# The last column block of a down projection in two passes by token tiles, on one core of a Trainium2 chip

## The reference, cut to what matters

```python
gate, up = jnp.split(h @ w_gu, 2, axis=-1)
f = (jax.nn.silu(gate) * up) @ w_down          # (640, 5632) @ (5632, 2048)
x = layer_norm(ALPHA * x + g2 * f, ln2_g, ln2_b)
# layer_norm: mean and variance over the 2048 columns of a token, then
# (x - mean) * rsqrt(var + eps) * g + b
```

## Time and profile before

| what | value |
|---|---|
| time, median of 3 runs | 2842.35 us (2841.35 to 2844.21) |
| profiled execution, its own time | 2838.47 us |
| its span, first to last instruction | 2836.7 us |
| busy: PE, DVE, ACT, POOL | 95%, 48%, 32%, 24% |
| a round of the down projection | 13.60 us, 44 of them |
| from the end of the last product to the end of the span | 31.2 us |

### The profile page before, as it was taken

How to read it: one execution, slowest core, us unless ns; L and a number is a source line. 1 busy time by engine, 2 the same in 40 slices (tenths; PEclk the granted TensorE clock), 3 DMA queues, 4 the chain that set the end, 5 groups by cost and what they waited for, 6 DMA issues and landing times.

```text
span 2836.7 us, 37630 instructions
## 1 busy us (share of the span) xinstructions
PE 2702.8 (95%) x16256; PEld 2412.5 (85%) x16256; DVE 1367.9 (48%) x1564; ACT 893.9 (32%) x933; POOL 680.5 (24%) x227
## 2 busy tenths in 40 slices
PE   5798999999998998999999999999999999999995
PEld 2577887879986885999999999999999888888884
DVE  5222232325566447555555555545555544445445
ACT  5222232323222116333333333333333322332231
POOL 0000000000000010444444444444433433333331
PEclk8999999999999997999999999999999999999998
DMA  8864545641346322223333332223333646454642
GB/s 328 316 238 176 184 170 198 212 150 58 106 150 238 101 74 103 86 94 98 103 104 104 104 103 88 94 95 104 104 104 122 245 180 220 171 204 168 217 167 104
DMA packets 164681, 424.50 MB, mean 150 GB/s; under 512 B 9484, under 2 KB 11924, under 8 KB 157476
## 3 DMA queue, kind: packets, MB, share of 16 engines
q1 hardware_dynamic: 162212, 416.84, 42.4%
q10 hardware_dynamic: 2304, 5.24, 0.5%
HBM read 388.20 MB, written 33.85 MB: 149 GB/s over the span
## 4 chain that ended last, share of the span: by engine, by line
PE 68%; DVE 9%; POOL 9%; DMA 8%; issue 3%; ACT 3%; SPq 0%; POOLq 0%; ACTq 0%; DVEq 0%
PE ps L1972 7%; PE ps L1974 7%; PE ps L1973 7%; PE ps L1947 6%; PE ps L1949 6%; PE ps L1948 6%; PE ps L1668 5%; PE ps L1670 5%; PE ps L1669 5%; DMA raw_w<-w_gu_b 4%; PE ps L1721 4%; POOL raw_w L785 3%; PE ps L1648 3%; DVE w_lo L1402 2%; POOL low L782 2%
## 5 line engine op out<-in xcount | busy, mean ns | idle before, releaser
L1402 DVE TENSOR_TENSOR w_lo<-raw_w,w_hi 128x1024 fp32r<-128x1024 f32 x264 | 332.7, 1260 | 295.6 <-ACT w_hi L1034 292.5
L1034 ACT ACTIVATE w_hi<-raw_w 128x1024 fp32r<-128x1024 f32 x264 | 269.5, 1054 | 604.9 <-POOL raw_w L791 367.8
L1947 PE MATMUL ps<-x_hi,w_hi 128*128 128x320 f32 x1408 | 437.2, 310 | 10.8 <-DVE w_lo L1402 8.9
L1948 PE MATMUL ps<-x_lo,w_hi 128*128 128x320 f32 x1408 | 436.7, 310 | 0.0
L1949 PE MATMUL ps<-x_hi,w_lo 128*128 128x320 f32 x1408 | 436.5, 310 | 0.0
L782 POOL TENSOR_TENSOR low<-raw_w 128x1024 f32<-128x1024 f32 x44 | 110.5, 2512 | 1052.4 <-DMA raw_w<-w_gu_b 926.1
L1512 DVE TENSOR_TENSOR x_lo<-low,x_hi 128x2560 fp32r<-128x2560 f32 x44 | 216.2, 4915 | 289.8 <-ACT x_hi L1100 289.8
L1668 PE MATMUL ps<-x_hi,w_hi 128*128 128x320 f32 x1056 | 341.7, 324 | 8.2 <-DVE x_lo L1206 6.2
L1972 PE MATMUL ps<-w_hi,x_hi 128*128 128x512 f32 x880 | 342.7, 389 | 2.4 <-POOL w_lo L796 2.4
L1974 PE MATMUL ps<-w_hi,x_lo 128*128 128x512 f32 x880 | 342.6, 389 | 0.0
L1973 PE MATMUL ps<-w_lo,x_hi 128*128 128x512 f32 x880 | 342.5, 389 | 0.0
(11 more groups left out here) (194 smaller groups left out, 4338.8 us busy)
## 6 DMA issues: line engine op xcount, KB each, us to landing
raw_w<-w_gu_b SPq DMA_DIRECT2D x176, 512.0 KB, 5.6
low<-w_ada SPq DMA_DIRECT2D x60, 1024.0 KB, 5.4
low<-hidden_scratch SPq DMA_DIRECT2D x44, 1280.0 KB, 6.0
raw_w<-w_down SPq DMA_DIRECT2D x44, 1024.0 KB, 5.1
raw_w<-w_in_b SPq DMA_DIRECT2D x33, 1024.0 KB, 7.4
high<-w_ada SPq DMA_DIRECT2D x22, 1024.0 KB, 5.3
raw_w<-w_out SPq DMA_DIRECT2D x16, 1024.0 KB, 5.1
x_raw<-w_ada SPq DMA_DIRECT2D x14, 1024.0 KB, 9.3
```

The source lines that it names most:

```text
L1034: nc.scalar.activation(weight(0, n), quad(W_OF[i]), ACT.Copy).then_inc(prod_hi, 1)
L1402: nc.vector.tensor_tensor(weight(1, n), quad(W_OF[n % 7]), weight(0, n).bitcast(F32), ALU.subtract).then_inc(prod_split, 1)
L1947: mm(prod_bank(n), wh, version(v, 0, k), start=k == 0, stop=False)
L1948: mm(prod_bank(n), wh, version(v, 1, k), start=False, stop=False)
```

## The change

The fourth column block is computed in two passes over the 11 groups. The first pass (rounds 33 to 43, LAST_A to LAST_B) takes token tiles 0 to 2, the second (rounds 44 to 54) tiles 3 and 4. There are 55 rounds in place of 44: the weight tiles of the block are loaded and split twice, the activation tiles in part each time (384 columns, then 256).

- In the second pass DVE makes `w_lo` (`late_rest`) in place of POOL, which splits up to round 44.
- While the second pass runs, the layer norm of tiles 0 to 2 is done: DVE evacuates tile 2 and makes the scale and the shift of the three (`scale_of`), ACT takes the roots and normalises the tiles (`tail_normalise`, one 128 x 2048 instruction each), and POOL multiplies by the gain and adds the bias (two 128 x 2048 instructions each, six in all). SP stores them after its last load.
- Tiles 3 and 4 are normalised on DVE after the last product, in halves of 1024 columns, and stored in halves.
- Gain and bias rows go into the free columns of the activation ring, loaded in round 37.

```diff
+N_DOWN = 5 * N_DG
+LAST_A, LAST_B = 3 * N_DG, 4 * N_DG
+TAIL = 3
+def down_unit(j):
+    b, g = divmod(j, N_DG)
+    return min(b, 3), g, ((0, TT), (0, TAIL), (TAIL, TT))[max(0, b - 2)]
...
+    x_rows = x_raw[:, 0:KT * T].rearrange("p (k c) -> p k c", c=T)
+    ln2_row = [x_rows[:, 8 * i:8 * i + 8, TAIL * P:T] for i in range(2)]
+    def folded_tile(t):
+        return u_acc[:, t, :].rearrange("p (k c) -> p k c", k=8)
...
         def load_down(j):
+            elif j - 2 <= LAST_B:
+                sp.wait_ge(split_done, FU + j - 1)
             else:
-                sp.wait_ge(split_done, FU + j - 1)
+                sp.wait_ge(late_split, j - 2 - LAST_B)
...
-        for t in range(TT):
-            sp.wait_ge(y_done, t + 1)
+        for t in range(TAIL):
+            sp.wait_ge(y_early, t + 1)
             sp.dma_start(y_t[t], u_acc[:, t, :]).then_inc(y_out, 16)
+        for t in range(TAIL, TT):
+            for i in range(2):
+                sp.wait_ge(y_done, 2 * (t - TAIL) + i + 1)
+                sp.dma_start(y_t[t][:, 1024 * i:1024 * i + 1024],
+                             u_acc[:, t, 1024 * i:1024 * i + 1024]).then_inc(y_out, 16)
...
     def _(pool):
-        for j in range(4 * N_DG):
+        for j in range(LAST_B + 1):
             s = (j + 1) % 2
             pool.wait_ge(down_hi, j + 1)
             nc.gpsimd.tensor_tensor(w_lo[:, s, :], raw_w[:, j % 2, :], w_hi[:, s, :].bitcast(F32),
                                     ALU.subtract).then_inc(split_done, 1)
+        pool.wait_ge(tail_rows_in, 32)
+        for t in range(TAIL):
+            tile = folded_tile(t)
+            pool.wait_ge(tail_normed, t + 1)
+            nc.gpsimd.tensor_tensor(tile, tile, ln2_row[0], ALU.mult).then_inc(y_gained, 1)
+            pool.wait_ge(y_gained, t + 1)
+            nc.gpsimd.tensor_tensor(tile, tile, ln2_row[1], ALU.add).then_inc(y_early, 1)
...
     def _(act):
+        for j in range(2, N_DOWN):
+            hid_round(j)
+            if j == LAST_B + 2:
+                tail_root(0)
+                tail_root(1)
+            if j > LAST_B + 2 and j - LAST_B - 3 < TAIL:
+                tail_normalise(j - LAST_B - 3)
+            down_round(j)
+            if j == LAST_B + 2:
+                tail_root(2)
...
     def _(dve):
+        def late_rest(j):
+            s = (j + 1) % 2
+            dve.wait_ge(down_hi, j + 1)
+            nc.vector.tensor_tensor(w_lo[:, s, :], raw_w[:, j % 2, :], w_hi[:, s, :].bitcast(F32),
+                                    ALU.subtract).then_inc(late_split, 1)
+        for nb in range(4):
+            for g in range(N_DG):
+                hid_rest(N_DG * nb + g + 2)
+                if g == 6:
+                    ready_rows(nb)
+            for t in range(TAIL - 1 if nb == 3 else TT):
+                evac_down(nb, t)
+        for j in range(LAST_B, N_DOWN):
+            if j + 1 < N_DOWN:
+                late_rest(j + 1)
+            if j == LAST_B:
+                evac_down(3, TAIL - 1)
+                scale_of(0)
+                scale_of(1)
+            if j == LAST_B + 1:
+                scale_of(2)
+            if j + 2 < N_DOWN:
+                hid_rest(j + 2)
+        for t in range(TAIL, TT):
+            evac_down(3, t)
...
+        for t in range(TAIL, TT):
+            tile = folded_tile(t)
...
+            for i in range(2):
+                part = slice(4 * i, 4 * i + 4)
+                link(nc.vector.scalar_tensor_tensor(tile[:, part], tile[:, part], mv(t, 0), ln2_row[0][:, part],
+                                                    ALU.subtract, ALU.mult))
+                nc.vector.scalar_tensor_tensor(tile[:, part], tile[:, part], mv(t, 2), ln2_row[1][:, part],
+                                               ALU.mult, ALU.add).then_inc(y_done, 1)
```

More of the change, by code:

```diff
@@ L748, in _ @@
         store_hid(FB - 2)
-        for j in range(4 * N_DG):
-            if j + 2 < 4 * N_DG:
+        for j in range(N_DOWN):
+            if j + 2 < N_DOWN:
                 load_hid(j + 2)
@@ L754, in _ @@
                 store_hid(FB - 1)
[L755 removed]
+            if j % N_DG == 2 and j < LAST_B:
                 load_down_rows(j // N_DG)
[L757 to L763 removed]
+            if j == LAST_A + 4:
+                sp.wait_ge(down_used, LAST_A)
+                for i in range(2):
+                    row = rows[4 + i:5 + i, :].rearrange("r (k c) -> r k c", k=8)
+                    sp.dma_start(ln2_row[i], row.to_broadcast([P, 8, 256])).then_inc(tail_rows_in, 16)
+        for t in range(TAIL):
+            sp.wait_ge(y_early, t + 1)
+            sp.dma_start(y_t[t], u_acc[:, t, :]).then_inc(y_out, 16)
+        for t in range(TAIL, TT):
[3 more added lines that the diff above has]
+                             u_acc[:, t, 1024 * i:1024 * i + 1024]).then_inc(y_out, 16)
+        sp.wait_ge(y_out, 16 * (2 * TT - TAIL))
     @block.gpsimd
@@ L1132, in _, with tail_root, tail_normalise @@
         down_round(1)
[L1133 to L1136, removed]
+        def tail_root(t):
             act.wait_ge(moments, TT + t + 1)
             nc.scalar.activation(mv(t, 2), mv(t, 1), ACT.Sqrt, bias=cols(C_EPS, 1)).then_inc(scaled, 1)
+        def tail_normalise(t):
+            act.wait_ge(tail_scale, t + 1)
+            nc.scalar.activation(u_acc[:, t, :], u_acc[:, t, :], ACT.Identity, bias=mv(t, 3),
+                                 scale=mv(t, 2)).then_inc(tail_normed, 1)
+        for j in range(2, N_DOWN):
[9 more added lines that the diff above has]
+        for t in range(TAIL, TT):
+            tail_root(t)
     @block.vector
@@ L1572, in stat2_of @@
             return stat2[:, t]
[L1574 to L1596, removed]
@@ L1597, in _, with ready_rows @@
+        def ready_rows(nb):
+            dve.wait_ge(down_gates_in, 80 * (nb + 1))
+            for i in range(2):
+                row = high[:, G_GATE + 512 * i:G_GATE + 512 * i + 512]
+                nc.vector.tensor_tensor(row, row, high[:, G_BIAS:G_BIAS + 512],
+                                        ALU.add).then_inc(down_gates, 1)
+            dve.wait_ge(down_gates, 2 * nb + 2)
+            dve.wait_ge(xn_in, 16 * (nb + 1))
             for t in range(TT):
-                i = TT * nb + t
@@ L1608, in _ @@
[L1608 to L1621, removed]
+                nc.vector.tensor_tensor(blk, blk, high[:, G_LN:G_LN + 512],
+                                        ALU.mult).then_inc(ln1_gained, 1)
@@ new lines, in _ @@
+        for t in range(TAIL, TT):
+            evac_down(3, t)
+        dve.wait_ge(tail_rows_in, 32)
+        for t in range(TAIL, TT):
+            tile = folded_tile(t)
+            dve.wait_ge(moments, TT + t + 1)
+            dve.wait_ge(scaled, t + 1)
+            link(nc.vector.reciprocal(mv(t, 2), mv(t, 2)))
+            for i in range(2):
+                part = slice(4 * i, 4 * i + 4)
[3 more added lines that the diff above has]
+                                               ALU.mult, ALU.add).then_inc(y_done, 1)
@@ L1950, in _ @@
             ins.then_inc(prod_done, 1)
[L1952 to L1955, removed]
+        for j in range(N_DOWN):
+            nb, g, tokens = down_unit(j)
+            s = (j + 1) % 2
+            if j <= LAST_B:
                 pe.wait_ge(split_done, FU + j + 1)
[L1957 to L1978, removed]
@@ new lines, in _ @@
+            else:
+                pe.wait_ge(late_split, j - LAST_B)
+            pe.wait_ge(hid_split, j + 1)
+            if j == 0:
+                pe.wait_ge(posted, 4 * FB - 3)
+            if j == N_DG:
+                pe.wait_ge(posted, 4 * FB)
+            for t in range(*tokens):
+                i = TT * nb + t
+                if g == 0 and i >= 8:
+                    pe.wait_ge(down_evac, i - 7)
+                for k in range(DG):
+                    rh = w_hi[:, s, k * 512:(k + 1) * 512]
+                    rl = w_lo[:, s, k * 512:(k + 1) * 512]
+                    at = (t - (TAIL if j >= LAST_B else 0)) * P
+                    xh = hid_slot(x_hi, j)[:, k, at:at + P]
+                    xl = hid_slot(x_lo, j)[:, k, at:at + P]
+                    begin, end = g == 0 and k == 0, g == N_DG - 1 and k == DG - 1
+                    mm(ps[:, (i + 5) % 8, :], xh, rh, start=begin, stop=False)
+                    mm(ps[:, (i + 5) % 8, :], xh, rl, start=False, stop=False)
+                    ins = mm(ps[:, (i + 5) % 8, :], xl, rh, start=False, stop=end)
+                if t == tokens[1] - 1:
+                    ins.then_inc(down_used, 1)
+                elif g == N_DG - 1:
+                    ins.then_inc(down_filled, 1)
```

59 lines of the change are left out of this document (43 added, 16 removed).

## The result

The changed kernel takes 2861.97 us (median of 4 runs, 2855.72 to 2863.41) against 2843.28 for the kernel before (4 runs): a ratio of 1.0062, 95% interval 1.0048 to 1.0076. It is slower, as forecast, by 17.6 us by the ratio (0.0062 times 2843.28) and 18.7 by the medians, where 10.8 were predicted. The median lies 1 us above the range of 2840 to 2861 and 5 above the forecast's own 2848 to 2857; by the ratio, counted from the 2842.35 of the prediction, it is 2860.0. The profiled execution took 2855.72, with a span of 2853.9, 17.2 above the span before.

The account below looks back on a forecast made before the run. PE, busy 95%, was taken to bound the kernel outside the tail. Losses of 1 + 1.3 + 1.2 + 20.2 + 2.3 = 26.0 us less 15.2 gained gave +10.8 on 2842.35: 2853 us, range 2840 to 2861, forecast's own 2848 to 2857.

Parts of the forecast that it names:

- The tail: Behind the last product: only two tiles left to normalise, in halves; 16.0 us in place of 31.2, 15.2 gained.
- Second pass, rounds 45 and 46: DVE's held hid_rest and its evacuations make w_lo late for PE: 1.3 and 1.2 us lost.
- The turns: POOL and DVE alternate in the second pass: three rounds of 12.2 us against PE's 5.44, 20.2 lost.
- The clock: After PE's idle gaps of 6.7 us, about 5 us at half speed; only behind round 49 it stays: 2.3 lost.
- Loads in runs of 1024 bytes: Second-pass activation tile in shorter runs: no loss taken; the rival that they cost as 2560 gave 2858, chance 0.08.
- The first pass: Rounds of 8.16 us: loads nothing late, DVE's block preparation held by POOL loses 0 to 2, taken as 1 us.
- one turn a round: Rival in the second pass: POOL gets one turn, rounds of 7.7 us six times, 13.6 lost; 2844, no change; chance 0.16.

Follow-up runs that it names:

- DVE version: Changed kernel with gain and bias on DVE, preparation in two, rows loaded later, first-layer-norm tile earlier, rounds 45 and 46 reordered: 2828.20 us, 0.9955 against the kernel before.
- halves: Changed kernel with POOL's six instructions as 12 of 1024 columns: 2847.74 us, ratio 1.0018 to the kernel before.
- quarters: Changed kernel with POOL's six instructions as 24 of 512 columns: 2835.61 us, ratio 0.9977 to the kernel before.
- gain on DVE: Changed kernel with POOL's six gain and bias instructions moved to DVE as twelve of 1024 columns: 2834.79 us, ratio 0.9981 to the kernel before.
- without POOL's six: Changed kernel with gain and bias left out for token tiles 0 to 2: 2833.29 us, ratio 0.9977 to the kernel before.

## Why the prediction was right, and where its size was off

- **The tail.** 15.2 us gained, predicted; 31.2 - 15.9 = 15.3 measured. A half tile took 1.28 us for 1.2 assumed.
- **Second pass, rounds 45 and 46.** `late_rest(45)` ends 6.45 us behind the end of round 43 (predicted 6.7), `late_rest(46)` 6.2 later (6.6): lost 1.0 and 0.7, for 1.3 and 1.2. With DVE's evacuations in another order nothing is lost there.
- **The turns.** 12.15, 12.08 and 12.09 us a round, predicted 12.2; lost 20.0, predicted 20.2. The rule of alternation came from one row, L1519, which had a single POOL instruction ahead of DVE; that it goes on with several in line was a guess from it. It held in all six turns, and at two other turn lengths. Only in the first turn two DVE operations went between POOL's, the shift and `x_lo` of round 47: POOL's second instruction was there only at 2770.52, when `x_lo` had begun. That POOL got two turns in round 47 hung on little: ACT had tile 0 ready at 2765.41, and `w_lo` of round 46 ended at 2765.96, 0.55 us later, where 0.9 were predicted.
- **The clock.** It fell at each of the three gaps and came back during the next round. Of the three gaps of some 6.5 us that the prediction named only the first was as long (6.4); the others were 3.5 and 4.7, since PE's slower rounds reached into them, which the wait swallowed as expected. From `w_lo` of round 49 (2802.28) to the last product are 35.7 us, six rounds are 32.6: some 3.0, predicted 2.3, since the clock stayed at half for 5.7 us of work there, where the prediction had taken about 5.
- **Loads in runs of 1024 bytes** cost PE nothing: in the DVE version it has no gap at 277 GB/s, though ACT was idle three times in the second pass (1.0, 0.5 and 3.5 us) until a weight tile landed. The Trainium skill, "DMA: Bandwidth & Descriptors", Specifications, gives line rate from 512 bytes up. The trace agrees as far as this rate goes.
- **The first pass** is the step that was mis-sized: 1 predicted ("between 0 and 2 us are lost there; I take 1", and of the loads "nothing late"), 5.7 measured. Its parts by the runs are three.
  - 2.4 for the preparation held twice by POOL, over the upper end of 2. Its length was right, 16.3 us (2716.91 to 2733.21); the slack was not. DVE began 0.5 us behind the end of round 39 (2716.39), since POOL had held `hid_rest(41)` ahead of it (4.61 us), and PE was through with round 41 at 2732.71, so the slack was 15.8 and not 16.3. And `hid_rest(42)` itself, 1.8 us, had no term in the sum.
  - 1.9 for the clock, which fell after this gap of 2.4 us, while the prediction had a price for it only in gaps of 6.7. In other kernels the same gap cost nothing by the clock, so this part may be absent in other executions.
  - 1.4 for weight tiles that landed late behind the block's burst, against windows that I had only compared with the sum of bytes ("nothing late").
- **Sum.** 5.7 + 24.8 - 15.3 = 15.2; 2.0 more had gone by before round 33, where both kernels issue the same work. In the other profiled kernels that place lies 0.1 to 4.6 us later than in the kernel before too. Its cause is open; it may be scatter between executions.

Of the rivals, that of one turn a round did not happen: the tile was normalised in time (the first POOL instruction came in ahead of `hid_rest(47)`), and while POOL had work, one of its instructions came between any two of DVE's subtractions.

## What to carry to other kernels

An idle engine is not free help if it shares something with the engine on the path: look in the trace for an operation of DVE that takes longer while POOL works, and take POOL's instruction length, not POOL's busy share, as the wait of each DVE instruction that reads two tiles in SBUF. Where both have to work, cut POOL's instructions until the turns of one round fit into its slack (here two of 1.0 to 1.1 us into 2.2), or give the work to DVE. When a round is made shorter, everything that was hidden once in a round, preparation of a block and bursts of loads, has to be laid against the new length.

## What the runs showed of the hardware that was not expected

- A DVE operation on a single column, with two inputs in SBUF, waited 4.40 us for POOL (the same operation took 2.17 with halves and 1.07 with quarters): the hold depends on POOL's instruction, not on DVE's size. Statistics and evacuations of 512 columns, with one input in SBUF, were not held, 0.69 us beside POOL as without it.
- The granted clock fell to half after PE's gap of 2.4 us ahead of round 42 in three kernels (changed, gain on DVE, halves) and stayed at full behind the same gap in two (quarters, without POOL's six). Within halves, PE's five gaps of 2.0 us in the second pass had it fall behind two. Behind the three long gaps of the changed kernel it was at half for 5.9, 3.4 and 5.7 us of work.
- The same kernel's runs lie 8 us apart (2855.72 to 2863.41), the profiled one the fastest, so the split by place above, and not the time, is what tells effects of 1 to 2 us apart.
